# One ring of ten slots for the expert weights of a hybrid encoder block, each item's w_down behind its own gate_up

## The chip, the cores and the metric

One core of one Trainium2 chip. The time is the device time of one execution in microseconds, the median of the runs. Everything is float32.

## What is computed

An encoder block for 256 tokens of width 1024: a Hyena branch and a differential attention, mixed into the residual, then a mixture of experts (32 experts, the best four for each token, SwiGLU), and a final norm. The change is in the mixture of experts and in the loads of its weights:

```python
logits = (hf @ w_router + b_router)
top_val, top_idx = lax.top_k(logits, TOP_K)          # 4 of 32
gates = jax.nn.softmax(top_val, axis=-1)
# for each expert e and the tokens xb routed to it
gu = xb @ w_gate_up[e] + b_gate_up[e]                # 1024 x 2048
gate, up = gu[:, :D_EXPERT], gu[:, D_EXPERT:]
gate = jnp.minimum(gate, 7.0)
up = jnp.clip(up, -7.0, 7.0)
glu = gate * jax.nn.sigmoid(1.702 * gate)
y = ((up + 1.0) * glu) @ w_down[e] + b_down[e]       # 1024 x 1024
out = out.at[row_tok].add(y * wts)
```

For one expert w_gate_up has 8 MB and w_down 4 MB, so all of them are 384 MB that come in once.

## The kernel before, in words

The kernel is written with explicit semaphores; every engine runs its own list of instructions in the order in which it is written, and no planner reorders anything.

**Front.** Up to about 300 us the projections, the Hyena branch, attention and the mix run. Their weights pass through a ring of six slots of 16 KB per partition (`ring`), one 2 MB transfer each, issued by SyncE in the order of the list `blocks`. The last six blocks are two of `w_in` (in8 and in9), `hy`, `att`, and two halves of `mix`.

**Items.** The mixture works on items of up to 64 tokens of one expert. An item of every expert comes first (32 of them), and further items follow only where an expert has more than 64 tokens. Here there are 32 items, taken in pairs, so `n_pairs` is 16 (`w_gate_up` is loaded 128 times). In a pair p, item A is 2p and item B is 2p+1.

For each pair TensorE does these pieces of work (lines of the profile in brackets):

- `gather(p)` (L788): picks the token rows of both items out of `xn` with a selection matrix `Sel`. The result in PSUM banks 7 and 6 is copied to `hTp` by `gathered(p)` (L1480), which signals `ga_sb`.
- `gate_up(p, s)` (L796 for the bias, L806 for 64 MATMULs): four pieces `j` of 2 MB of `w_gate_up`; each piece, when read, counts up `gu_used`.
- `activate` on VectorE (L1431 to L1435) with a sigmoid on ScalarE (L1070), then `act_transpose` on TensorE (L812) and `act_copy` on ScalarE (L1074), which gives `actT`.
- `down` (L824, 32 MATMULs): two pieces of 2 MB of `w_down`, counted by `dn_used`. The result in bank 6 is copied by `y_copy` (L1470) into one half of `y`.
- `place_weights` (L841): transposes the matrix of gate weights `Wt`, which `placed` (L1485) copies to `Pw`.
- `scatter` (L833): adds the pair's rows onto the token sums in banks 0 to 3.

**Order around the change.** Before, `down` runs one item late. In the loop over the pairs 1 to 15 TensorE does: gather(p), gate_up A(p), down of item B of pair p-1, transposes of A, gate_up B(p), scatter of the pair before, down A(p), transposes of B, place_weights. The last down stands behind the loop.

**Slots.** There are ten slots of 2 MB: `gu_a` (four slots of the ring, for the w_gate_up of A), `gu_b` (four slots made of the regions dft, ur and x that the front no longer needs, for the w_gate_up of B) and `dn_row` (two slots of the ring, for every w_down). Each row is refilled as its own piece is read. SyncE's loop issues, in this order, four of gate_up A, two of w_down of B of the pair before, four of gate_up B, two of w_down of A. An issue waits for `gu_used` or `dn_used`, and all that stands behind it in SyncE's list waits too. The last w_down goes in four pieces of 1 MB into `last_row`.

**Loops.** TensorE and SyncE have one loop body for the pairs: TensorE's runs for 1 to 15, SyncE's for 2 to 15, with expert numbers from the table `table_i`. VectorE and ScalarE have a loop for 1 to 15.

Of the kernel before, what the change touches and what calls it, by code (L numbers as in the profile page):

```python
# [33 lines left out]
D = 1024  # L34
# [66 lines left out]
def build(nc, a, out):  # L101
    with ExitStack() as ctx:
# [40 lines left out]
        gu_a = ring[:NJ]  # L143
        gu_b = [span("dft", 0, 4096), span("ur", 4096, 4096), span("ur", 0, 4096), span("x", 0, 4096)]
        dn_row = ring[NJ:NJ + NC]
        last_row = [at("ring", 2048 * c, 2048) for c in range(4)]
        fgB = at("ring", 4096 * 2, D)
        junk = at("ring", 4096 * 3, 2048)
# [104 lines left out]
        def sem(name):  # L253
            return ctx.enter_context(nc.semaphore(name))
# [11 lines left out]
            gu_used dn_used tr_done sc_done ga_done pt_done  # L266
# [4 lines left out]
        s_gua = [sem(f"gate_up_a_in{j}") for j in range(NJ)]  # L271
        s_gub = [sem(f"gate_up_b_in{j}") for j in range(NJ)]
        s_dn = [sem(f"down_in{c}") for c in range(NC)]
# [53 lines left out]
        w_gu, w_dn = a["w_gate_up"], a["w_down"]  # L327
        block = ctx.enter_context(nc.Block())
# [3 lines left out]
        def _(sp):  # L332
# [33 lines left out]
            def gate_up(dst, landed, expert, j):  # L366
# [5 lines left out]
            def down(c, expert):  # L372
                src = w_dn[expert, c] if isinstance(expert, int) else w_dn[bass.ds(expert, 1), c]\
                    .rearrange("o p n -> p (o n)")
                sp.dma_start(dn_row[c], src).then_inc(s_dn[c], 16)


            last_use = {n % 6: n for n in range(len(blocks))}
            for f in sorted(range(6), key=lambda s: last_use[s]):
                if blocks[last_use[f]] == ("mix", 0, 0):  # L380
                    sp.wait_ge(S["s_ps"], 2 * HEADS)
                    gate_up(gu_b[0], s_gub[0], 1, 0)
                    sp.wait_ge(S["pj_sb"], KD)
                    gate_up(gu_b[1], s_gub[1], 1, 1)
                    sp.dma_start(b_down[0:E, :], a["b_down"][0]).then_inc(S["bd_in"], 16)
                wait_used(blocks[last_use[f]])
                if f < NJ:
                    gate_up(gu_a[f], s_gua[f], 0, f)
                else:
                    down(f - NJ, 0)  # L390
            sp.wait_ge(S["mix_ps"], 4)
            gate_up(gu_b[2], s_gub[2], 1, 2)
# [1188 lines left out]
```

## Time and profile before

| | us |
|---|---|
| median of 3 runs | 1252.24 |
| lowest, highest | 1250.06, 1254.26 |
| the profiled execution, whole | 1254.92 |
| its span in the trace | 1253.1 |
| TensorE busy (MATMUL) | 1140.6 |
| VectorE busy | 451.5 |
| ScalarE busy | 116.4 |
| bytes moved | 465.13 MB, 371 GB/s over the span |

The profile divides the span into 40 slices of 31.3 us each. Its chain of work that ended last lists 52% TensorE and 40% transfers of w_gate_up. A share of busy time is a mean over stages that have different limits, so the stages must be read apart. Two hold for this kernel: the front up to about 360 us, and the pairs behind it.

### The profile page before, as it was taken

Reading aid. Unit: us, or ns where it says so; the run is one execution under the profiler, and the core shown is the slowest. Engines: PE = TensorE matmul, PEld = TensorE weight load, DVE = VectorE, ACT = ScalarE, POOL = GpSimd, SP = SyncE. Lnnn points to the kernel's source line nnn. Section 1 sums busy time; section 2 is a strip of 40 time slices with the busy share of each in tenths; the row PEclk is TensorE's granted clock in tenths of the full one; section 3 lists DMA queues with packets and bytes.
Section 4 is the critical chain, followed back from the end, with each engine's and each line's share of the span. In section 5 each row is a group of like instructions: output and inputs, shape, how many; then the busy total and the mean of one; then the engine's idle time right before and its main releaser. Section 6 shows DMA issues by size and latency. Waiting matters only on the chain.

```text
span 1253.1 us, 13746 instructions
## 1 busy us (share of the span) xinstructions
PE 1140.6 (91%) x5333; PEld 521.6 (42%) x5333; DVE 451.5 (36%) x975; ACT 116.4 (9%) x217; POOL 11.8 (1%) x12
## 2 busy tenths in 40 slices
PE   3999999997999999999999999998989898999996
PEld 1588678864333333333232323232333333232322
DVE  3467236527613141432313141313233231313143
ACT  1111122611000000000000000000000000000000
POOL 0000000003000000000000000000000000000000
PEclk9999999998999999999999999999999999999999
DMA  9997941167659999999999999999999999999994
GB/s 341 366 370 303 391 163 68 67 248 292 269 212 429 428 427 429 428 429 428 428 428 429 429 427 428 427 430 429 427 428 427 430 429 427 428 427 430 428 428 190
DMA packets 49025, 465.13 MB, mean 371 GB/s; under 512 B 5466, under 2 KB 6220, under 8 KB 21100
## 3 DMA queue, kind: packets, MB, share of 16 engines
q1 hardware_dynamic: 45592, 461.11, 88.3%
q10 hardware_dynamic: 3412, 3.74, 1.0%
q8 instruction: 13, 0.21, 0.1%
q14 instruction: 8, 0.07, 0.0%
HBM read 463.79 MB, written 1.05 MB: 371 GB/s over the span
## 4 chain that ended last, share of the span: by engine, by line
PE 52%; DMA 40%; DVE 4%; SPq 2%; issue 1%; ACT 1%; DVEq 0%; ACTq 0%
DMA arena<-in_w_gate_up 40%; PE ps L806 12%; PE ps L824 11%; PE ps L566 8%; PE ps L833 5%; PE ps L689 2%; PE ps L712 2%; PE ps L661 2%; PE ps L788 1%; SPq L370 1%; PE ps L560 1%; PE ps L483 1%; PE ps L529 1%; PE ps L796 1%; PE ps L516 1%
## 5 line engine op out<-in xcount | busy, mean ns | idle before, releaser
L806 PE MATMUL ps<-arena 128*64 128x512 f32 x2048 | 455.2, 597 | 33.9 <-DMA arena<-in_w_gate_up 33.9
L806 PEld LDWEIGHTS ps<-arena 128*64 128x64 f32 x2048 | 141.4, 137 | 345.9 <-issue 273.2
L824 PE MATMUL ps<-arena 128*64 128x512 f32 x1024 | 226.0, 594 | 0.7 <-issue 0.7
L1431 DVE TENSOR_SCALAR arena<-ps 128x512 f32<-128x512 f32 x32 | 22.1, 691 | 380.2 <-PE ps L806 380.2
L824 PEld LDWEIGHTS ps<-arena 128*64 128x64 f32 x1024 | 72.1, 137 | 149.3 <-issue 146.0
L1470 DVE TENSOR_TENSOR arena<-ps,arena 64x512 f32<-64x512 f32 x64 | 44.1, 689 | 188.5 <-PE ps L824 188.1
L566 PE MATMUL ps<-arena 128*128 128x256 f32 x448 | 97.7, 380 | 0.0
L566 PEld LDWEIGHTS ps<-arena 128*128 128x128 f32 x448 | 85.1, 190 | 13.8 <-issue 2.6
L1070 ACT ACTIVATE arena<-arena 128x512 f32<-128x512 f32 x32 | 20.1, 630 | 607.3 <-DVE arena L1431 607.3
L788 PE MATMUL ps<-arena 128*128 128x128 f32 x512 | 63.1, 283 | 10.8 <-DVE arena L1485 10.8
L788 PEld LDWEIGHTS ps<-arena 128*128 128x128 f32 x512 | 60.1, 197 | 14.7 <-issue 14.7
L833 PE MATMUL ps<-arena 128*128 128x512 f32 x128 | 59.3, 605 | 1.5 <-DVE arena L1470 1.5
L796 PE MATMUL ps<-arena 32*64 32x512 f32 x256 | 35.3, 621 | 12.9 <-DVE arena L1480 12.9
L1456 DVE TENSOR_SCALAR arena<-arena 128x128 f32<-128x128 f32 x128 | 44.3, 346 | 4.6
L1074 ACT ACTIVATE arena<-ps 128x512 f32<-128x512 f32 x32 | 19.1, 597 | 248.0 <-PE ps L812 248.0
L1480 DVE COPY arena<-ps 128x512 f32<-128x512 f32 x32 | 22.1, 692 | 52.7 <-PE ps L788 52.7
L833 PEld LDWEIGHTS ps<-arena 128*128 128x128 f32 x128 | 23.0, 189 | 37.6 <-issue 35.2
L1445 DVE SCALAR_TENSOR_TENSOR arena<-arena 128x128 f32<-128x128 f32 x96 | 33.8, 352 | 3.4
L661 PE MATMUL ps<-arena 128*128 128x256 f32 x128 | 32.1, 409 | 0.0
L1220 DVE SCALAR_TENSOR_TENSOR arena<-arena 128x2048 f32<-128x2048 f32 x12 | 28.2, 2351 | 3.1 <-DMA arena<-in_w_ada 2.7
L689 PE MATMUL ps<-arena 128*128 128x256 f32 x128 | 28.0, 380 | 0.0
L712 PE MATMUL ps<-arena 128*128 128x512 f32 x64 | 27.8, 593 | 0.0
(240 smaller groups left out, 629.5 us busy)
## 6 DMA issues: line engine op xcount, KB each, us to landing
arena<-in_w_gate_up SPq DMA_DIRECT2D x128, 2048.0 KB, 31.3
arena<-in_w_down SPq DMA_DIRECT2D x62, 2048.0 KB, 23.6
arena<-in_w_ada SPq DMA_DIRECT2D x12, 2048.0 KB, 17.1
arena<-in_w_in SPq DMA_DIRECT2D x10, 2048.0 KB, 16.5
arena<-in_w_mix_out SPq DMA_DIRECT2D x2, 2048.0 KB, 8.9
arena<-in_w_down SPq DMA_DIRECT2D x4, 1024.0 KB, 28.5
arena<-in_w_hy_out SPq DMA_DIRECT2D x1, 2048.0 KB, 15.0
arena<-in_w_attn_out SPq DMA_DIRECT2D x1, 2048.0 KB, 19.0
```

The source lines that it names most:

```text
L566: last = mm(bank(b, 256, c * 256), w[:, k, cc * P:(cc + 1) * P], hT[:, k, :], start=(k == 0), stop=(k == KD - 1))
L661: last = mm(bank(m % 3, 256, (i % 2) * 256), w[:, k, cc * P:(cc + 1) * P], hT[:, k, :], start=(k == 0), stop=(k == KD - 1))
L689: last = mm(bank(pj_bank[i % 4], 256, o), w[:, k, i * P:(i + 1) * P], src[:, k, :], start=(k == 0), stop=(k == CT - 1))
L712: return mm(bank(2 * t + h), merged[:, k, t * P:(t + 1) * P], mix[k // 4][:, k % 4, h * 512:(h + 1) * 512], start=(k == 0), stop=(k == KD ...
L788: last = mm(bank(b, 128, kk * 128), xn[:, t, k * P:(k + 1) * P], Sel[:, t, :], start=(t == 0), stop=(t == TT - 1))
L796: mm(ps[64 * h:64 * h + 64, 4 + b, :], mask[E * b:E * b + E, s, :], sel_bias[E * b:E * b + E, h * 512:(h + 1) * 512], start=True, stop=False)
L806: last = mm(ps[64 * h:64 * h + 64, 4 + b, :], hTp[:, k, s * 64:(s + 1) * 64], w[:, o:o + 512], start=False, stop=(k == KD - 1))
L824: last = mm(ps[64 * h:64 * h + 64, 6, :], lhs, rows[c][:, qq * D + h * 512:qq * D + (h + 1) * 512], start=(q == 0), stop=(q == 7))
L833: last = mm(bank(2 * t + h), Pw[:, t, :], y[:, h * 512:(h + 1) * 512], start=False, stop=stop, skip_group_check=True)
L1445: ins = V.scalar_tensor_tensor(Sel[:, t, :], iota, s, Sel[:, t, :], ALU.is_equal, ALU.add)
L1456: st(V.tensor_scalar(dst[:, t, :], iota, pk[:, k, t:t + 1], gk[:, k, t:t + 1], ALU.is_equal, ALU.mult))
L1470: last = V.tensor_tensor(y[64 * s:64 * s + 64, 512 * h:512 * (h + 1)], ps[64 * h:64 * h + 64, 6, :], gate2B[64 * h:64 * h + 64, 512 * h:51 ...
```

## The change

All ten slots become one ring, `slots`, in the order of use: for each pair four of gate_up A, two of w_down A, four of gate_up B, two of w_down B. Transfer n goes to slot n mod 10. One semaphore, `consumed`, counts the pieces that TensorE has read, in the same order. Down of an item follows its own gate_up: TensorE does gate_up A, scatter of the pair before, transposes of A, down A, gate_up B, gather of the next pair, transposes of B, place_weights, down B. `gathered` for the pairs from 1 on moves from VectorE to ScalarE (`ACT.Copy`). On VectorE, `y_copy` stands ahead of `activate`. The pairs 1 to 14 are written out on TensorE and SyncE, and only pair 15 (and further ones) is in a loop, whose w_down B goes in four pieces of 1 MB into the slots of w_down A of the same pair, in every run of the loop. The first slots are handed to the expert weights in another order: gate_up 0 first, then its w_down, then gate_up 1.

TensorE from the first gate_up on, before (a row `MATMUL x32` in this list stands for 64 MATMULs of the profile, `x16` of L824 and L788 for 32; L855 and L861 add b_down):

```order
L806 MATMUL ps<-arena 64x512 x32
L855 MATMUL ps<-arena 32x128 x2
L861 MATMUL ps<-arena 128x512 x4
L812 MATMUL ps<-arena 128x128 x4
L796 MATMUL ps<-arena 64x512 x4
L806 MATMUL ps<-arena 64x512 x32
L824 MATMUL ps<-arena 64x512 x16
L812 MATMUL ps<-arena 128x128 x4
L841 MATMUL ps<-arena 128x128 x2
```

And after, where the lines are L846 (gate_up), L852 (act_transpose), L864 (down), L835 (bias), L827 (gather), L881 (place_weights):

```order
L846 MATMUL ps<-arena 64x512 x32
L895 MATMUL ps<-arena 32x128 x2
L901 MATMUL ps<-arena 128x512 x4
L852 MATMUL ps<-arena 128x128 x4
L864 MATMUL ps<-arena 64x512 x16
L835 MATMUL ps<-arena 64x512 x4
L846 MATMUL ps<-arena 64x512 x32
L827 MATMUL ps<-arena 128x128 x16
L852 MATMUL ps<-arena 128x128 x4
L881 MATMUL ps<-arena 128x128 x2
L864 MATMUL ps<-arena 64x512 x16
```

Down of expert 0 moved from behind the second gate_up to ahead of it, and the gather of pair 1 stands between the second gate_up and its transposes.

A later pair on TensorE, before (the loop body, without its register instructions):

```order
L806 MATMUL ps<-arena 64x512 x32
L833 MATMUL ps<-arena 128x512 x4
L819 REGISTER_ALU
L824 MATMUL ps<-arena 64x512 x16
L812 MATMUL ps<-arena 128x128 x4
L841 MATMUL ps<-arena 128x128 x2
```

And after (one of the written-out pairs, L873 is scatter):

```order
L835 MATMUL ps<-arena 64x512 x4
L846 MATMUL ps<-arena 64x512 x32
L873 MATMUL ps<-arena 128x512 x4
L852 MATMUL ps<-arena 128x128 x4
L864 MATMUL ps<-arena 64x512 x16
L835 MATMUL ps<-arena 64x512 x4
L846 MATMUL ps<-arena 64x512 x32
L827 MATMUL ps<-arena 128x128 x16
L852 MATMUL ps<-arena 128x128 x4
L881 MATMUL ps<-arena 128x128 x2
L864 MATMUL ps<-arena 64x512 x16
```

Scatter moved from the second gate_up of a pair to the first, and the gather from the pair's start to its second gate_up.

SyncE from the last block of the front on, before:

```order
L360 DMA arena<-in_w_mix_out 128x4x1024 x2
L370 DMA arena<-in_w_gate_up 128x4096 x2
L375 DMA arena<-in_w_down 128x4096 x2
L370 DMA arena<-in_w_gate_up 128x4096 x2
L385 DMA arena<-in_b_down 32x1024
L370 DMA arena<-in_w_gate_up 128x4096 x8
L375 DMA arena<-in_w_down 128x4096 x2
L370 DMA arena<-in_w_gate_up 128x4096 x4
L375 DMA arena<-in_w_down 128x4096 x2
```

And after (L393 is w_gate_up, L399 w_down):

```order
L382 DMA arena<-in_w_mix_out 128x4x1024 x2
L393 DMA arena<-in_w_gate_up 128x4096 x4
L399 DMA arena<-in_w_down 128x4096 x2
L413 DMA arena<-in_b_down 32x1024
L393 DMA arena<-in_w_gate_up 128x4096 x4
L399 DMA arena<-in_w_down 128x4096 x2
L393 DMA arena<-in_w_gate_up 128x4096 x4
L399 DMA arena<-in_w_down 128x4096 x2
```

The w_down of expert 1 now comes ahead of the w_gate_up of expert 2, and each of its transfers waits for a piece of expert 0's gate_up to be read; the number of transfers issued at each place up to there is the same, ten slots and four refills.

The core of the diff:

```diff
+        in8, in9, hy, att, mix0, mix1 = (ring[where[b] % 6] for b in blocks[-6:])
+        slots = [in8, span("dft", 0, 4096), in9, hy, att, span("ur", 4096, 4096), mix0, mix1,
+                 span("ur", 0, 4096), span("x", 0, 4096)]
+        NS = len(slots)
+        A0, DA, B0, DB, PAIR = 0, NJ, NJ + NC, 2 * NJ + NC, 2 * (NJ + NC)
+        FIXED = E // 2 - 1
+        fixed_slot = [(PAIR * FIXED + i) % NS for i in range(DB)]
+        uses_before = [sum(n % NS == k for n in range(PAIR * FIXED)) for k in range(NS)]
+        def place(p, i):
+            if isinstance(p, int):
+                n = PAIR * p + i
+                return slots[n % NS], s_slot[n % NS], 16 * (n // NS + 1)
+            k = fixed_slot[i]
+            return slots[k], s_slot[k], p * 16 + 16 * (uses_before[k] + 1 - FIXED)
...
+            def free(p, i):
+                sp.wait_ge(S["consumed"], used(p, i - NS + 1))
-            def pair_of(p, e_a, e_prev, e_b):
+            def pair_of(p, e_a, e_b):
                 for j in range(NJ):
-                    sp.wait_ge(S["gu_used"], p * 8 + (j - 7))
-                    gate_up(gu_a[j], s_gua[j], e_a, j)
+                    free(p, A0 + j)
+                    gate_up(place(p, A0 + j), e_a, j)
                 for c in range(NC):
-                    sp.wait_ge(S["dn_used"], p * 4 + (c - 3))
-                    down(c, e_prev)
+                    if isinstance(p, int):
+                        free(p, DA + c)
+                    else:
+                        sp.wait_ge(S["consumed"], used(p, c - 1))
+                    down(place(p, DA + c), e_a, c)
                 for j in range(NJ):
-                    sp.wait_ge(S["gu_used"], p * 8 + (j - 3))
-                    gate_up(gu_b[j], s_gub[j], e_b, j)
-                for c in range(NC):
-                    sp.wait_ge(S["dn_used"], p * 4 + (c - 1))
-                    down(c, e_a)
+                    free(p, B0 + j)
+                    gate_up(place(p, B0 + j), e_b, j)
+                if isinstance(p, int):
+                    for c in range(NC):
+                        free(p, DB + c)
+                        down(place(p, DB + c), e_b, c)
+                else:
+                    for c in range(4):
+                        sp.wait_ge(S["consumed"], used(p, DA + c // 2 + 1))
+                        sp.dma_start(piece(c), w_dn[bass.ds(e_b, 1), c // 2, :, 2048 * (c % 2):2048 * (c % 2 + 1)]
+                                     .rearrange("o p n -> p (o n)")).then_inc(s_last[c], 16)
...
+            def down_a(p):
                 pe.wait_ge(S["act_rdy"], p * 2 + 1)
                 act_transpose()
+                pe.wait_ge(S["actT_rdy"], p * 2 + 1)
+                down([place(p, DA + c) for c in range(NC)])
+            def gate_up_b(p):
                 gate_up(p, 1)
+                pe.wait_ge(S["y_rdy"], p * 2 + 1)
+                gather(p + 1)
+            def down_b(p):
+                pe.wait_ge(S["ga_sb"], p * 2 + 3)
                 pe.wait_ge(S["act_rdy"], p * 2 + 2)
                 act_transpose()
                 pe.wait_ge(S["actT_rdy"], p * 2 + 2)
                 pe.wait_ge(S["wt_rdy"], p + 1)
                 place_weights()
+                pe.wait_ge(S["ga_sb"], p * 2 + 4)
...
+            def pair_of(p):
+                pe.wait_ge(S["mask_rdy"], p + 1)
+                gate_up(p, 0)
+                pe.wait_ge(S["y_rdy"], p * 2)
+                pe.wait_ge(S["pt_sb"], p)
+                scatter(False)
+                down_a(p)
+                gate_up_b(p)
+                down_b(p)
+            for p in range(1, FIXED):
+                pair_of(p)
+            with pe.Fori(FIXED, n_pairs) as p:
+                pair_of(p)
...
+            def gathered(p):
+                for half in range(2):
+                    act.wait_ge(S["ga_done"], p * 2 + (half + 1))
+                    A(hTp[:, 4 * half:4 * half + 4, :].rearrange("p k s -> p (k s)"), ps[:, 7 - half, :], ACT.Copy)\
+                        .then_inc(S["ga_sb"], 1)
+            def pair_of(p):
+                sigmoid(p * 2)
+                act_copy(p * 2)
+                sigmoid(p * 2 + 1)
+                gathered(p + 1)
+                act_copy(p * 2 + 1)
```

## Rows read from the trace of the kernel before

**Rows 1.** The page: busy time by engine, and GB/s in 40 slices.

```profile
PE 1140.6 (91%) x5333; PEld 521.6 (42%) x5333; DVE 451.5 (36%) x975; ACT 116.4 (9%) x217; POOL 11.8 (1%) x12
...
GB/s 341 366 370 303 391 163 68 67 248 292 269 212 429 428 427 429 428 429 428 428 428 429 429 427 428 427 430 429 427 428 427 430 429 427 428 427 430 428 428 190
```

**Rows 2.** Chain of waits, two of 11 alike: start us, us, what.

```profile
878.91 41.95 DMA arena<-in_w_gate_up
...
937.64 41.96 DMA arena<-in_w_gate_up
```

**Rows 3.** Timeline of TensorE, one early pair: start us, us, instructions [idle <-releaser].

```profile
419.64 3.83 PE L788 MATMUL ps<-arena 128*128 128x128 f32 x32 [0.70 <-DVE arena L1485]
...
446.61 1.09 PE L796 MATMUL ps<-arena 32*64 32x512 f32 x8
447.63 13.95 PE L806 MATMUL ps<-arena 128*64 128x512 f32 x64
461.51 3.71 PE L833 MATMUL ps<-arena 128*128 128x512 f32 x8
465.15 7.09 PE L824 MATMUL ps<-arena 128*64 128x512 f32 x32
472.17 0.66 PE L812 MATMUL ps<-arena 128*128 128x128 f32 x4
473.51 0.44 PE L841 MATMUL ps<-arena 128*128 128x128 f32 x2 [0.69 <-ACT arena L1074]
474.70 0.48 PE L788 MATMUL ps<-arena 128*128 128x128 f32 x2 [0.75 <-DVE arena L1485]
```

**Rows 4.** Stretches of 5 us: each engine busy, PEclk, DMA share, GB/s.

```profile
335.00:340.00 5.00, 5.00 (x20) 1.62 (x18) 4.20 (x11) 1.83 (x3) 0.00 (x0) 0.91 1.02 436
340.00:345.00 5.00, 5.00 (x22) 1.61 (x20) 4.01 (x13) 0.00 (x0) 0.00 (x0) 0.75 0.92 393
345.00:350.00 5.00, 5.00 (x26) 1.67 (x24) 0.00 (x0) 0.00 (x0) 0.00 (x0) 1.00 0.00 0
...
355.00:360.00 5.00, 5.00 (x26) 1.68 (x24) 2.77 (x4) 0.63 (x1) 0.00 (x0) 1.00 0.25 46
360.00:365.00 5.00, 3.46 (x19) 1.42 (x16) 2.03 (x4) 0.60 (x1) 0.00 (x0) 1.00 0.85 341
```

**Rows 5.** Timeline of SyncE, issue of the 15th transfer.

```profile
358.67 0.33 SPq L375 DMA_DIRECT2D arena<-in_w_down  x1
```

**Rows 6.** Timeline of all engines, from expert 0's activation on.

```profile
337.98 0.66 PE L812 MATMUL ps<-arena 128*128 128x128 f32 x4
...
338.68 0.60 ACT L1074 ACTIVATE arena<-ps 128x512 f32<-128x512 f32 x1 [2.44 <-PE ps L812]
...
340.07 15.13 PE L806 MATMUL ps<-arena 128*64 128x512 f32 x64
...
355.03 7.03 PE L824 MATMUL ps<-arena 128*64 128x512 f32 x32
```

**Rows 7.** Timeline of all engines, at the end.

```profile
1214.61 3.65 PE L806 MATMUL ps<-arena 128*64 128x512 f32 x16 [1.25 <-DMA arena<-in_w_gate_up]
...
1218.32 0.69 DVE L1431 TENSOR_SCALAR arena<-ps 128x512 f32<-128x512 f32 x1 [10.16 <-PE ps L806]
...
1220.50 0.69 DVE L1435 TENSOR_TENSOR arena<-arena 128x512 f32<-128x512 f32 x1
...
1231.29 7.09 PE L824 MATMUL ps<-arena 128*64 128x512 f32 x32 [0.65 <-issue]
...
1238.42 1.39 DVE L1470 TENSOR_TENSOR arena<-ps,arena 64x512 f32<-64x512 f32 x2 [7.32 <-PE ps L824]
```

**Rows 8.** Stretches of 2.5 us at the end, columns as in rows 4.

```profile
1232.50:1235.00 2.50, 2.50 (x14) 0.89 (x12) 0.00 (x0) 0.00 (x0) 0.00 (x0) 1.00 0.43 175
```

**Rows 9.** w_gate_up transfers between 700 and 1100: issue to landing.

```profile
DMA to landing us min/median/max: 26.9/34.4/42.0
```

**Rows 10.** The page: instruction queue, packets, MB, share of 16 engines.

```profile
q8 instruction: 13, 0.21, 0.1%
```

More of the change, by code:

```diff
@@ L142, in build @@
         NJ, NC = 4, 2
[L143 to L148, printed above, removed]
         y = b_down = span("prm", 0, D)
@@ L327, in build, with piece, used @@
         w_gu, w_dn = a["w_gate_up"], a["w_down"]
+        in8, in9, hy, att, mix0, mix1 = (ring[where[b] % 6] for b in blocks[-6:])
[12 more added lines that the diff above has]
+            return slots[k], s_slot[k], p * 16 + 16 * (uses_before[k] + 1 - FIXED)
+        def piece(c):
+            return slots[fixed_slot[DA + c // 2]][:, 2048 * (c % 2):2048 * (c % 2 + 1)]
+        def used(p, i):
+            return p * PAIR + i
+        fgB = slots[fixed_slot[A0]][:, 0:D]
+        junk = slots[fixed_slot[A0 + 1]][:, 0:2048]
         block = ctx.enter_context(nc.Block())
@@ L370, in gate_up, with down @@
                 sp.dma_start(dst, src).then_inc(landed, 16)
-            def down(c, expert):
+            def down(place_, expert, c):
+                dst, landed, _ = place_
                 src = w_dn[expert, c] if isinstance(expert, int) else w_dn[bass.ds(expert, 1), c]\
                     .rearrange("o p n -> p (o n)")
[L375 to L390, printed above, removed]
+                sp.dma_start(dst, src).then_inc(landed, 16)
+            wait_used(blocks[-6])
+            gate_up(place(0, 0), 0, 0)
+            sp.wait_ge(S["s_ps"], 2 * HEADS)
+            gate_up(place(0, 1), 0, 1)
+            wait_used(blocks[-5])
+            gate_up(place(0, 2), 0, 2)
+            wait_used(blocks[-4])
+            gate_up(place(0, 3), 0, 3)
+            down(place(0, DA), 0, 0)
+            sp.wait_ge(S["pj_sb"], KD)
+            down(place(0, DA + 1), 0, 1)
+            sp.dma_start(b_down[0:E, :], a["b_down"][0]).then_inc(S["bd_in"], 16)
+            wait_used(blocks[-2])
+            gate_up(place(0, B0), 1, 0)
+            wait_used(blocks[-1])
+            gate_up(place(0, B0 + 1), 1, 1)
             sp.wait_ge(S["mix_ps"], 4)
-            gate_up(gu_b[2], s_gub[2], 1, 2)
+            gate_up(place(0, B0 + 2), 1, 2)
             sp.wait_ge(S["res_ps"], 1)
@@ L413, in expert_of @@
             def expert_of(index):
                 return sp.value_load(table_i[0:1, bass.ds(index, 1)], min_val=0, max_val=E - 1)
-            pair_of(1, 2, 1, 3)
+            for c in range(NC):
+                free(0, DB + c)
+                down(place(0, DB + c), 1, c)
+            for p in range(1, FIXED):
+                pair_of(p, 2 * p, 2 * p + 1)
             sp.wait_ge(S["tables"], 2)
             n_pairs = sp.value_load(table_i[0:1, 48:49], min_val=E // 2, max_val=ITEMS // 2)
-            with sp.Fori(2, n_pairs) as p:
-                pair_of(p, expert_of(p * 2), expert_of(p * 2 - 1), expert_of(p * 2 + 1))
+            with sp.Fori(FIXED, n_pairs) as p:
+                pair_of(p, expert_of(p * 2), expert_of(p * 2 + 1))
@@ L813, in act_transpose, with down @@
                 last.then_inc(S["tr_done"], 1)
-            def down(landed, rows, count):
-                n = KD // len(rows)
-                for c in range(len(rows)):
-                    pe.wait_ge(landed[c], count)
+            def down(pieces):
+                n = KD // len(pieces)
+                for c, (rows, landed, count) in enumerate(pieces):
+                    pe.wait_ge(landed, count)
                     for qq in range(n):
@@ L1476, in gathered @@
                     v.wait_ge(S["ga_done"], p * 2 + (half + 1))
-                    if half and isinstance(p, int):
+                    if half:
                         v.wait_ge(S["ex_ps"], 1)
```

130 lines of the change are left out of this document (50 added, 80 removed).

## The prediction

> **What bounds the kernel now.** I read the page first: TensorE is busy for 91% of the span, yet from slice 13 of 40 on the GB/s row stands at 427 to 430 in every slice [rows 1]. Both could be the limit, so the next view is the chain of waits, in order of time. It goes, once in each pair of experts, through one wait for a w_gate_up transfer of 42 us, and these waits are 58.73 us apart [rows 2]. A pair moves 12 transfers of 2 MB (8 of w_gate_up, 4 of w_down), 25.17 MB, and 25.17 MB in 58.73 us is 428 GB/s: one transfer every 4.895 us. Early on, while TensorE is still behind, the same pair takes 55.06 us from gather to gather (419.64 to 474.70) [rows 3]. So TensorE needs 55 us for what the stream delivers in 58.7 us, and after some 530 us it only follows the stream. From there the end is: the moment from which the stream runs without a hole, plus the bytes that are left at 428 GB/s, plus what is computed after the last byte.
>
> The moment is what matters. The table of 5 us stretches shows DMA shares of 0.92, 0.00, 0.25 and 0.85 for 340-345, 345-350, 355-360 and 360-365 (350-355 reads 0.00 too) [rows 4]. That is 0.4 + 5 + 5 + 3.75 + 0.75 = 14.9 us in which the engines of the stream stand still. SyncE issues the next w_down at 358.67 [rows 5], because its destination is the slot of expert 0's w_down, and TensorE reads that only from 355.03 on, after the whole gate_up of expert 1 (340.07 to 355.2) [rows 6]. By then 14 of the 192 transfers (counting 2 MB each) are in: ten slots filled, and the first four refilled. The other 178 follow without a hole.
>
> At the end, the last w_gate_up piece lets its matmuls start at 1214.61, the last down runs from 1231.29 to 1238.4, and the stream is dry at about 1233.6 (share 0.43 in 1232.5-1235) [rows 7, 8]. From the end of the last down to the end of the span are 14.7 us.
>
> **1. The hole at 345 closes: -14.5 us.** The change lets down of expert 0 follow its own gate_up. The transposes L812 start at 337.98, the copy L1074 ends at 338.68 + 0.60 = 339.28 [rows 6], so down can start at 339.35. Half of it, 16 of 32 matmuls, frees a slot: 3.5 us by 7.09 us for 32 [rows 3]. The granted clock here is 0.91 and then 0.75 of full on average over 335-345 [rows 4], and the 64 matmuls of L806 at 340.07 took 15.13 us [rows 6] where they take 13.95 otherwise [rows 3], so add up to 1.2 us. The slot is free at 342.9 to 344.1, while the stream is busy with the four refills until 344.6. The queue never runs dry, or for a fraction of a microsecond until the first packets flow. Of 14.9 us, 13.4 to 14.9 are recovered; I take 14.5.
>
> Does the hole come back later? In a ring of ten, transfer n (from 0) needs use n-10 read. With the stream running from 345.0, transfer 16 wants to start at 355 and needs the first piece of expert 1's gate_up read: down ends at 347.4, four bias matmuls and 16 matmuls later it is 352. Transfer 20 wants 374.4 and needs the first half of expert 1's down: gate_up ends at 362.5, gather 3.83, transposes, copy and place_weights 2.2, half a down 3.5, so 372. Transfer 26 wants 403.8 and needs expert 2's down: 399. The margin is about 3 us in each place, and later grows by 3.9 us a pair (next part). That margin covers the estimate; if it were used up, the hole would be as large as the excess.
>
> **2. TensorE's pair in the new order: 54.8 us, nothing on the path.** The work is the same; what differs is which matmuls cover the activation. Expert A: bias and gate_up 14.9 (446.61 to 461.51), scatter 3.64, transposes to the end of the copy 1.34 (472.17 to 473.51), down 7.02 [rows 3]. Expert B: 14.9, gather 3.83, 1.34, place_weights and its successor 0.44 to 1.09 (0.8), down 7.02 [rows 3]. Sum 54.8 us, against 58.73 us of the stream. VectorE's chain L1431 to L1435 takes 2.9 us (1218.32 to 1220.50 + 0.69) [rows 7]; scatter's 3.64 and gather's 3.83 cover it. If they did not, 2.9 us twice in a pair would still only reach 60.6. The two copies of the gathered rows go from VectorE to ScalarE, 0.6 us each by L1074 [rows 6]; the second one ends behind the gather and ahead of the activation's copy, which puts some tenths on the switch. All of it lies under waits for the stream, once the first pairs are over.
>
> SyncE passes its queue in the order of use: in the last pair w_down waits for the last down of the pair before, and the four half pieces wait for down of expert 30. Behind each of these waits at least four transfers are in flight, 19.6 us, while the waiting takes under 10 us. Up to 42 us from issue to landing (8.6 transfers) are there already before the change [rows 9], so the deeper queue is not new.
>
> **3. The tail: +2.7 us.** Before, four w_down transfers follow the last w_gate_up piece (experts 30 and 31); after, only the two of expert 31. So the last w_gate_up piece comes 2 x 4.895 = 9.8 us later against the stream: 1224.4 where it was 1214.6. Then 16 matmuls 3.6, the gather 3.85 (issued for a pair that doesn't exist), transposes and copy 1.34, place_weights 0.8, down 7.1: its end is 1241.1, where it was 1238.4. The last quarter of w_down, in at 1233.6 as before, isn't waited for. Bounds 2.3 and 3.0 by the two values for place_weights. Before, the 9.4 us of scatter, down and switch lay between; they now lie ahead of it.
>
> **4. Code: +2.0 us.** Fourteen pairs are written out on TensorE where before one loop body served. Each has 258 MATMULs and as many weight loads. Before, the 5333 MATMULs [rows 1] come from 5333 - 14 x 258 = 1721 written ones, and the page lists 13 packets of 0.21 MB on the instruction queue [rows 10]: one packet of 16 KB for 132 of them. So 27 packets more, 0.44 MB, which is 1.0 us of the stream's rate. A packet occupies one of the 16 engines: 0.1% of 16 x 1253 us (0.05 to 0.15) over 13 packets is 0.8 to 2.3 us. Spread over all engines 27 of them cost 1.4 to 3.9 us. I take 2.0, near the lower end and to the plain rate. Below nothing it can't go, since the stream holds all the old bytes too; the lower bound is 0.
>
> The Trainium skill (Runtime: NRT & Kernel Launch, Instruction fetch mechanics) says the sequencer fetches its code in blocks of 16 KiB over a queue of its own and that the cost of crossing a block is "mostly hidden". The 13 packets of 0.21 MB agree with the size; by the word "hidden" this term would be 0 and the time 1240. That stays inside the forecast's own range. The skill (DMA: Bandwidth & Descriptors, queues and rings) also has each DMA engine take turns between its queues packet by packet, so that a fetch would take its own time out of one engine's stream; no run here shows yet how fetches spread over the engines.
>
> **Sum.** -14.5 + 2.7 + 2.0 = -9.8 us. The profiled execution took 1254.92 us (span 1253.1, 1.8 around it), so 1245.1 for its like; it lies 2.7 above the median of 1252.24, so the median goes to 1242.4. With the bounds: -14.9 + 2.3 + 0 = -12.6 and -13.4 + 3.0 + 3.9 = -6.5, so 1239.6 to 1245.7. The stream's rate reads between 427 and 430 from slice to slice, 0.35% either way of 871 us, so 3 us more on both sides.
>
> **Rivals.**
> Fetches fall on one engine (slower). With a share of 1.0 and one transfer behind the other, each transfer must be spread over all 16 engines, and it is in when the slowest has done its part. If the 27 extra packets always take the same engine, that one is late by 27 x 0.8 = 22 to 62 us. At 1 us a packet: -11.8 + 27 = +15, 1267. It decides from 0.44 us of stream per packet on (11.8 / 27). For it: the packets are few, one queue. Against it, weakly: the slices right behind the last written-out code (13 and 14, 429 and 428) read no lower than the later ones [rows 1]. A mix (four or five engines) would give +6 in place of +2, 1246 to 1248.
>
> TensorE becomes the bound (no gain). If the switches expose the chain wholly, the pair is 54.8 + 5.8 = 60.6, which is 1.9 us x 14 = 26 us over the stream, less 11.8: 1266. With half of it, 57.7, nothing shows. Break-even at 59.6 us a pair (58.73 + 11.8 / 14). Against it: the covers of 3.64 and 3.83 stand in the rows.
>
> The hole moves (gain partly lost). If the margins of 3 us are misjudged by 8 us in one of the first pairs, 5 us come back: 1247; if they are missed in several, within 0.3%.
>
> The change gives the full 14.5 with a free tail and free code: 1238.
>
> **Chances.** Forecast (1237 to 1247) 0.70; the full gain 0.05; the mix or a moved hole 0.11, of which 0.06 end at 1246 to 1248.5 and 0.05 within 0.3% of before; one engine slowed 0.10 and TensorE the bound 0.04, which together give 0.11 slower and 0.03 within 0.3%. 0.3% is 3.8 us, about what this kernel's measurement can tell from no change: faster means under 1248.5, slower over 1256. So faster 0.81, the same 0.08, slower 0.11. The range 1237 to 1252 leaves out the slower cases and the last part of the full gain.
>
> **What will show it.** The table of 5 us stretches should have DMA share near 1.0 from 325 on through 345-365; if a hole stands there, step 1 fails. SyncE's issue of the 15th transfer should come at 343 to 344. In the steady part pairs should be 58.7 to 58.9 us apart; 60 or more is the code or TensorE, told apart by whether TensorE waits for w_gate_up (code) or VectorE and ScalarE (the switch). The instruction queue should list about 40 packets. From the end of the last w_gate_up matmuls to the end of the last down should be 13 us. Wrong altogether would be a GB/s row below 425 in the middle slices.

## Result and the profile after

| | median us | lowest, highest |
|---|---|---|
| before | 1252.01 | 1250.06, 1254.26 |
| changed | 1243.70 | 1242.74, 1244.79 |

The ratio is 0.9933, interval 0.9914 to 0.9953, so 8.3 us faster. In a later comparison the changed kernel took 1244.93 against 1251.99, ratio 0.9943 (0.993 to 0.9956). The profiled execution of the changed kernel took 1242.74, with a span of 1240.9.

The page of the changed kernel (busy time, GB/s, instruction queue), which answers to [rows 1, 10]:

```profile
PE 1133.0 (91%) x5365; PEld 519.7 (42%) x5365; DVE 427.9 (34%) x945; ACT 133.8 (11%) x249; POOL 11.8 (1%) x12
...
GB/s 341 369 398 305 394 146 68 136 208 270 277 417 429 428 427 428 428 428 426 427 430 427 426 429 427 428 428 426 428 427 429 428 427 427 428 427 427 429 424 135
...
q8 instruction: 42, 0.69, 0.2%
```

The slice that read 212 GB/s before reads 417. TensorE's share is the same 91%, and says nothing of what changed.

The 5 us stretches of the changed kernel (from, to and length in us, busy time of TensorE, its weight loads, VectorE, ScalarE and GpSimd, granted clock, DMA share, GB/s, as in [rows 4]):

```profile
335.00:340.00 5.00, 5.00 (x18) 1.41 (x16) 4.44 (x14) 0.00 (x0) 0.00 (x0) 0.71 0.98 419
340.00:345.00 5.00, 5.00 (x28) 1.39 (x26) 1.38 (x2) 0.00 (x0) 0.00 (x0) 1.00 0.82 292
345.00:350.00 5.00, 5.00 (x26) 1.67 (x24) 0.00 (x0) 0.00 (x0) 0.00 (x0) 1.00 1.02 436
350.00:355.00 5.00, 5.00 (x26) 1.64 (x24) 0.00 (x0) 0.00 (x0) 0.00 (x0) 1.00 1.00 429
355.00:360.00 5.00, 5.00 (x32) 2.70 (x29) 1.65 (x3) 0.63 (x1) 0.00 (x0) 1.00 0.99 423
360.00:365.00 5.00, 4.26 (x32) 3.00 (x33) 1.69 (x4) 1.68 (x3) 0.00 (x0) 1.00 1.01 433
```

A hole is best counted in the bytes that are missing, since a starting stream has a share before it has its rate. At 428 GB/s six stretches would sum to 2568. Here they sum to 2432, and 136 / 428 x 5 = 1.6 us are missing. Before, the same six sum to 1216 (436, 393, 0, 0, 46, 341), which is 15.8 us. So 14.2 us came back.

TensorE of the changed kernel around that place, and at the end of the program, and SyncE's issue of the 15th transfer:

```profile
314.99 13.95 PE L846 MATMUL ps<-arena 128*64 128x512 f32 x64
...
334.70 8.63 PE L864 MATMUL ps<-arena 128*64 128x512 f32 x32 [0.69 <-ACT arena L1123]
```

```profile
339.95 3.76 SPq L393 DMA_DIRECT2D arena<-in_w_gate_up  x2
```

```profile
1210.13 3.65 PE L846 MATMUL ps<-arena 128*64 128x512 f32 x16 [1.25 <-DMA arena<-in_w_gate_up]
1213.72 3.84 PE L827 MATMUL ps<-arena 128*128 128x128 f32 x32
1217.39 0.60 PE L852 MATMUL ps<-arena 128*128 128x128 f32 x4
1218.73 0.44 PE L881 MATMUL ps<-arena 128*128 128x128 f32 x2 [0.74 <-ACT arena L1123]
1219.10 7.09 PE L864 MATMUL ps<-arena 128*64 128x512 f32 x32
```

**The zero of the clock.** The front before the experts is the same in both kernels, but it does not end at the same time in every execution. The first 64 MATMULs of gate_up start at 319.61 before and at 314.99 in this execution; in the second profiled execution of the same changed kernel they start at 320.39, and its span is 1246.2. From that start to the end of the span are 925.9 and 925.8 us. So I compare this rest, span less start, which repeats within 0.1 us where whole executions differ by 5 (within 0.6 us in the two traces of a kernel of experiment 5, 923.2 and 923.8). The kernel before has one trace. Before it is 1253.1 - 319.61 = 933.5. The change moved it by -7.6.

### The profile page after: what moved, and what is told of

Same layout as the page of the kernel before. It is cut to its first block, busy times and chain, and to the rows that moved or that the text cites. A ratio compares the mean times of both kernels' runs of the same rounds, so it can differ in the third digit from the quotient of the medians.

```text
span 1240.9 us, 13121 instructions
## 1 busy us (share of the span) xinstructions
PE 1133.0 (91%) x5365; PEld 519.7 (42%) x5365; DVE 427.9 (34%) x945; ACT 133.8 (11%) x249; POOL 11.8 (1%) x12
## 4 chain that ended last, share of the span: by engine, by line
PE 60%; DMA 33%; DVE 3%; ACT 2%; SPq 1%; issue 1%; DVEq 0%; ACTq 0%
DMA arena<-in_w_gate_up 31%; PE ps L846 18%; PE ps L864 13%; PE ps L605 8%; PE ps L827 5%; DMA arena<-in_w_ada 2%; PE ps L728 2%; PE ps L751 2%; PE ps L873 2%; PE ps L700 2%; PE ps L835 1%; PE ps L599 1%; ACT arena L1123 1%; ACT arena L1130 1%; PE ps L881 1%; PE ps L640 1%
## 5 line engine op out<-in xcount | busy, mean ns | idle before, releaser
L846 PE MATMUL ps<-arena 128*64 128x512 f32 x2048 | 454.8, 596 | 36.5 <-DMA arena<-in_w_gate_up 36.3
L846 PEld LDWEIGHTS ps<-arena 128*64 128x64 f32 x2048 | 140.8, 137 | 348.3 <-issue 274.1
L864 PE MATMUL ps<-arena 128*64 128x512 f32 x1024 | 228.3, 599 | 11.0 <-ACT arena L1123 11.0
L864 PEld LDWEIGHTS ps<-arena 128*64 128x64 f32 x1024 | 71.1, 138 | 146.5 <-issue 131.7
L605 PE MATMUL ps<-arena 128*128 128x256 f32 x448 | 97.7, 379 | 0.0
L605 PEld LDWEIGHTS ps<-arena 128*128 128x128 f32 x448 | 84.9, 190 | 14.0 <-issue 2.5
L827 PEld LDWEIGHTS ps<-arena 128*128 128x128 f32 x544 | 63.8, 196 | 13.4 <-issue 13.4
L827 PE MATMUL ps<-arena 128*128 128x128 f32 x544 | 67.0, 283 | 0.0
L873 PE MATMUL ps<-arena 128*128 128x512 f32 x128 | 59.3, 605 | 1.5 <-DVE arena L1526 1.5
L873 PEld LDWEIGHTS ps<-arena 128*128 128x128 f32 x128 | 23.0, 189 | 37.6 <-issue 35.3
L835 PE MATMUL ps<-arena 32*64 32x512 f32 x256 | 34.8, 612 | 1.2 <-DVE arena L1536 1.2
L700 PE MATMUL ps<-arena 128*128 128x256 f32 x128 | 29.0, 380 | 0.0
L728 PE MATMUL ps<-arena 128*128 128x256 f32 x128 | 28.0, 379 | 0.0
L728 PEld LDWEIGHTS ps<-arena 128*128 128x128 f32 x128 | 24.2, 190 | 3.2
L700 PEld LDWEIGHTS ps<-arena 128*128 128x128 f32 x128 | 23.8, 190 | 2.9
## 6 DMA issues: line engine op xcount, KB each, us to landing
arena<-in_w_hy_out SPq DMA_DIRECT2D x1, 2048.0 KB, 14.9
```

The costliest lines, as they stand in the source:

```text
L605: last = mm(bank(b, 256, c * 256), w[:, k, cc * P:(cc + 1) * P], hT[:, k, :], start=(k == 0), stop=(k == KD - 1))
L700: last = mm(bank(m % 3, 256, (i % 2) * 256), w[:, k, cc * P:(cc + 1) * P], hT[:, k, :], start=(k == 0), stop=(k == KD - 1))
L728: last = mm(bank(pj_bank[i % 4], 256, o), w[:, k, i * P:(i + 1) * P], src[:, k, :], start=(k == 0), stop=(k == CT - 1))
L827: last = mm(bank(b, 128, kk * 128), xn[:, t, k * P:(k + 1) * P], Sel[:, t, :], start=(t == 0), stop=(t == TT - 1))
L835: mm(ps[64 * h:64 * h + 64, 4 + b, :], mask[E * b:E * b + E, s, :], sel_bias[E * b:E * b + E, h * 512:(h + 1) * 512], start=True, stop=False)
L846: last = mm(ps[64 * h:64 * h + 64, 4 + b, :], hTp[:, k, s * 64:(s + 1) * 64], w[:, o:o + 512], start=False, stop=(k == KD - 1))
```

## Experiments

**1. The order alone.** In the kernel before, only pair 0's down of expert 0 is put ahead of the second gate_up; the slots stay in rows.

```diff
-            gate_up(0, 1)
             pe.wait_ge(S["actT_rdy"], 1)
             down(s_dn, dn_row, 16)
+            gate_up(0, 1)
```

> The kernel before, with one part of the change alone: in the first pair, down of expert 0 stands ahead of the gate_up of expert 1. The ten slots stay split into 4 + 4 + 2. Theory A (the split of the slots, not the order alone, makes the hole): w_down of expert 1 is now issued near 344 and the hole at 345 closes, but after it and four w_gate_up transfers (6 x 4.9 = 29 us, to about 374) the next transfer in SyncE's list is a w_down again, whose slot is read only by the down of expert 1, near 388. So a hole of about 14 us appears at 375 to 389 and the time stays within 2 us of before, about 1252. Rival B (the order alone brings the gain): no hole comes back, the stream starts 14 us earlier, and with the tail of before the time is 1238.

Measured: 1258.43 against 1252.29, ratio 1.0047 (1.0032 to 1.0061). Its stretches, and SyncE's next w_down:

```profile
340.00:345.00 5.00, 5.00 (x28) 1.50 (x28) 1.25 (x4) 0.00 (x0) 0.00 (x0) 1.00 0.82 269
...
370.00:375.00 5.00, 4.21 (x30) 2.29 (x30) 0.79 (x2) 0.00 (x0) 0.00 (x0) 0.97 0.53 223
375.00:380.00 5.00, 5.00 (x26) 1.63 (x24) 0.00 (x0) 0.00 (x0) 0.00 (x0) 1.00 0.00 0
380.00:385.00 5.00, 5.00 (x26) 1.65 (x24) 0.00 (x0) 0.00 (x0) 0.00 (x0) 1.00 0.00 0
385.00:390.00 5.00, 5.00 (x26) 1.71 (x24) 2.45 (x4) 0.63 (x1) 0.00 (x0) 1.00 0.00 0
390.00:395.00 5.00, 5.00 (x28) 1.77 (x28) 1.00 (x2) 0.11 (x1) 0.00 (x0) 1.00 0.65 210
```

```profile
390.88 3.76 SPq L375 DMA_DIRECT2D arena<-in_w_down  x2
```

```profile
362.85 0.66 PE L812 MATMUL ps<-arena 128*128 128x128 f32 x4 [2.97 <-DVE arena L1435]
...
365.59 6.06 PE L788 MATMUL ps<-arena 128*128 128x128 f32 x32 [0.71 <-DVE arena L1485]
```

The hole at 345 is gone and one of 20 us stands 30 us later, where the two slots of w_down wait for down of expert 1 behind another gate_up. The rest behind the start is 939.2, 5.7 longer than before; the missing bytes grow from 15.8 to 21.8 us (1.8 before 350 and 20.0 from 370 to 400), which accounts for it. Down behind its own gate_up closes no hole by itself in this slot plan. Theory A had the hole right and its size wrong (14 us, 1252 in time). Measured from the start of the experts, down of expert 1 comes 6.2 us later than before: nothing stands any more between gate_up and transposes of expert 1, so TensorE waits 2.97 us for its activation, and the gather behind it takes 6.06 us in place of 3.83 (granted clock 0.50 in 365-370, which is 1.2 GHz). So the uncovered activation makes up most of the 6 us; the hole that comes back would cost about what the first one did.

**2. The ring without the new order in pair 0.** In the changed kernel, pair 0 keeps the old work order (VectorE's order in that pair follows it), and the ring brings its transfers in the order in which that uses them.

```diff
-                n = PAIR * p + i
+                n = PAIR * p + (i if p else LATE[i])
...
-            down_a(0)
-            gate_up_b(0)
+            pe.wait_ge(S["act_rdy"], 1)
+            act_transpose()
+            gate_up(0, 1)
+            pe.wait_ge(S["actT_rdy"], 1)
+            down([place(0, DA + c) for c in range(NC)])
```

`LATE` is (0, 1, 2, 3, 8, 9, 4, 5, 6, 7, 10, 11).

> The changed kernel, with the first pair in the old order of work: gate_up of expert 1 ahead of down of expert 0, and the ring and its list in that order too. Theory A (the ring alone closes the hole, since the next slot to be read is always the next to be filled): transfer 15 waits for the first piece of expert 1's gate_up, read near 340 + 3.9 = 344 on the clock of before, and the stream has no hole over 2 us there; time within 1.5 us of the changed kernel, 1243 to 1245. Rival B (down right behind its gate_up is what is needed): a hole of 10 us or more at 340 to 360, time 1252 or more.

Measured: 1247.82 against 1252.29, ratio 0.9947 (0.993 to 0.9965). Its stretches:

```profile
345.00:350.00 5.00, 5.00 (x26) 1.61 (x24) 0.00 (x0) 0.00 (x0) 0.00 (x0) 1.00 0.80 269
350.00:355.00 5.00, 5.00 (x26) 1.68 (x24) 0.00 (x0) 0.00 (x0) 0.00 (x0) 1.00 1.04 446
```

No hole beyond the same 1.7 us, and 926.4 behind its start, 0.5 longer than the changed kernel. Its median lies above the expected range; its profiled execution started the experts at 319.8, so most of that is the front, though I can't show this for the executions without a trace. Together with experiment 1: the ring, with slots filled and freed in the order of use, closes the hole, and the place of expert 0's down does not matter to it. In the ring the 15th transfer needs a piece of gate_up read, whichever work comes first.

**3. Nearly no written-out pairs.** FIXED from 15 to 1, so every pair from 1 on is in the loop.

```diff
-        FIXED = E // 2 - 1
+        FIXED = 1
```

> The changed kernel with all pairs from 1 on in the loop. The least code (about 13 packets), but w_down A of each pair waits for the last down of the pair before while TensorE is still some 28 us behind. Theory A (the ring in the order of use matters until TensorE has caught up): holes in the stream in the pairs 1 to 3, 12 us or more in sum, and a time of 1249 or more. Rival B (order of use matters only in the first pair): 1240.

Measured: 1259.81 against 1251.90, ratio 1.0065 (1.0038 to 1.0092), the slowest of all. The instruction queue lists 14 packets in place of 42. Stretches and SyncE:

```profile
350.00:355.00 5.00, 5.00 (x26) 1.72 (x24) 0.00 (x0) 0.00 (x0) 0.00 (x0) 1.00 0.70 298
355.00:360.00 5.00, 5.00 (x24) 1.44 (x21) 0.00 (x0) 0.00 (x0) 0.00 (x0) 1.00 0.00 0
360.00:365.00 5.00, 4.28 (x38) 4.04 (x36) 2.90 (x5) 2.31 (x4) 0.00 (x0) 1.00 0.00 0
365.00:370.00 5.00, 4.99 (x24) 1.84 (x26) 0.42 (x1) 0.00 (x0) 0.00 (x0) 1.00 0.02 5
```

```profile
369.21 3.76 SPq L399 DMA_DIRECT2D arena<-in_w_down  x2
```

In the loop the w_down of A waits not for the slot ten transfers back but for down of the pair before (`used(p, c - 1)`): 369.2 is the middle of down of expert 1. From 335 to 380 the bytes of 19.2 us are missing, 3.4 more than before. With the tail (+2.1) and 15 pairs at 0.15 (experiment 5) that gives +7.8; measured are 941.2 - 933.5 = +7.7. So the written-out pairs are there for the early waits, not for TensorE.

**4. The price of code.** In the kernel before, TensorE's pairs 1 to 14 (or 1 to 7) are written out, nothing else.

```diff
-            with pe.Fori(1, n_pairs) as p:
+            def pair_of(p):
...
+            for p in range(1, 15):
+                pair_of(p)
+            with pe.Fori(15, n_pairs) as p:
+                pair_of(p)
```

> The kernel before, with TensorE's loop written out for the pairs 1 to 14, and nothing else. 27 to 29 more instruction packets. Theory A (fetching the code takes stream time, as the 59.1 us a pair of the changed kernel against 58.73 suggests): pairs of about 59.1 us, +4 to +5 us, 1256 to 1257. Rival B (fetches hidden): pairs stay at 58.73, time 1252. Rival C (only their bytes count): +1.0 us, 1253.

> The kernel before, with TensorE's pairs 1 to 7 written out and 8 to 15 in the loop: half the dose of the run that wrote out 14 (+5.1 us, 59.1 us a pair). Theory A (each packet of code costs stream time): about 27 to 28 packets on the instruction queue, +2.5 us, pairs 8 to 15 back at 58.73 us apart. Rival B (the cost is that of having more code, whenever it runs, or of the first pairs only): all of the +5 or none, or pairs 8 to 15 slow too.

Measured: 14 pairs 1257.36 against 1252.29, ratio 1.0033 (1.0020 to 1.0046), 42 packets; 7 pairs 1255.85 against 1251.90, ratio 1.0022 (1.0008 to 1.0035), 28 packets. The chain of waits with 14 pairs written, and then with 7, of which the first three rows here belong to written pairs:

```profile
700.11 42.73 DMA arena<-in_w_gate_up
759.63 41.94 DMA arena<-in_w_gate_up
818.36 42.40 DMA arena<-in_w_gate_up
```

```profile
584.99 42.88 DMA arena<-in_w_gate_up
644.66 42.55 DMA arena<-in_w_gate_up
704.00 41.93 DMA arena<-in_w_gate_up
762.72 41.95 DMA arena<-in_w_gate_up
```

Written pairs are 59.1 us apart on average, looped ones 58.74. By the medians 29 packets cost 5.1 us, 0.18 each, and 15 cost 3.9, 0.26 each (the interval allows 0.07 to 0.29); by the rest behind the start they cost 5.5 and 1.8, 0.19 and 0.12 each.

The trace holds more than these sums. The semaphore of a 2 MB transfer counts up 16 times, once as each sixteenth of it lands, and every count has its time. In the kernel before, the last count of a transfer comes 2.0 to 2.2 us behind the first, from 407 us to the end, and both repeat every 4.895 us. With written-out pairs each code packet moves exactly one of the 16 counts back by 1.53 us, and the other 15 stay within 0.03 us. Followed from transfer to transfer in the kernel with 14 pairs, it is one of the same eight counts each time, in the same order, three and a half times round. The other eight lose nothing, and the first count still comes every 4.895 us. But a transfer is in when its last count is, so the stream that TensorE sees moves back by as much as the slowest of the eight: 1.53 us for a round of eight packets, 0.19 each. From 407 us to the last w_gate_up the last counts lose 5.6 us with 14 pairs written (28 packets in that stretch; first to last count grows from 2.0 to 7.6 us), 2.0 us with 7 (14 packets, to 4.0 us) and 0.1 us in the kernel before. That is the rest behind the start within 0.2 us, and it says why 15 packets cost less each: a packet costs nothing where it meets a sixteenth that is not the slowest.

**5. Fewer written pairs in the changed kernel.** FIXED = 10, then FIXED = 5.

```diff
-        FIXED = E // 2 - 1
+        FIXED = 5
```

> The changed kernel with the pairs 1 to 9 written out and 10 to 15 in the loop (before: 1 to 14 and 15). In the loop both w_down of a pair use the same two slots, so w_down A waits for the last down of the pair before; by then TensorE follows the stream and four or more transfers are in flight. Theory A (29 packets of code cost 4.5 us, 0.16 us each): 10 packets fewer, -1.6 us, 1242; pairs 10 to 15 at 58.73 us apart. Rival B (the code costs nothing): unchanged, 1243.7. Rival C (the loop's wait makes holes): each pair of the loop 2 us or more longer, 1250 or more.

> The changed kernel with the pairs 1 to 4 written out and 5 to 15 in the loop, on all engines' lists of TensorE and SyncE. 21 packets of code fewer. TensorE is then still behind the stream when the loop begins, by about 9 us at pair 5 (it gains 4.7 us a pair and has caught up in pair 6 or 7), and w_down A of the loop waits for the last down of the pair before, behind which 16 us of transfers are in flight. Theory A (code 0.18 us a packet, wait covered): -3 us against the changed kernel, less about 1 us for the quarters of w_down that the loop moves in 1 MB pieces (58.85 against 58.74 us a pair in the run with 10), so 1241 to 1242. Rival B (the lag is larger than that cover): holes of several us in the pairs 5 and 6, 1245 or more. Rival C (code isn't what costs): 1244.

Measured: 1244.42, ratio 0.9927 (0.9911 to 0.9944), 32 packets; 1244.05, ratio 0.9932 (0.9911 to 0.9952), 22 packets. Theory A had 1242 and 1241 to 1242; the medians show no gain over the changed kernel. Part of the reason is in the chain of the second one:

```profile
934.87 40.42 DMA arena<-in_w_gate_up
993.76 40.46 DMA arena<-in_w_gate_up
```

The looped pairs are 58.88 us apart, not 58.74. A looped pair brings 4 of its 25 MB in four transfers of 1 MB. One more kernel tells whether the pieces cost that: it brings them in two transfers of 2 MB.

```diff
-                    for c in range(4):
-                        sp.wait_ge(S["consumed"], used(p, DA + c // 2 + 1))
-                        sp.dma_start(piece(c), w_dn[...]).then_inc(s_last[c], 16)
+                    for c in range(NC):
+                        sp.wait_ge(S["consumed"], used(p, DA + c + 1))
+                        down((slots[fixed_slot[DA + c]], s_last[c], None), e_b, c)
```

> The kernel with the pairs 5 to 15 in the loop, and w_down B in the loop in two transfers of 2 MB instead of four of 1 MB. Theory A (1 MB pieces cost 0.1 us a pair): 58.74 us a pair in the loop, 1 us under the run with four pieces, 1240 to 1241; the last down starts 9 us after the last w_gate_up piece is in, when the first 2 MB are in, so the tail doesn't change. Rival B (pieces cost nothing): the same as the run with four.

Measured: 1242.76 against 1251.90, ratio 0.9923 (0.9902 to 0.9943). Its chain:

```profile
932.02 40.28 DMA arena<-in_w_gate_up
990.77 40.31 DMA arena<-in_w_gate_up
```

58.74 us apart again. The pieces cost 0.14 us a pair, 1.5 us in the 11 looped pairs of FIXED = 5, whose rest behind the start is 924.8. Without the pieces it is 923.2 us, 2.7 less than in the changed kernel, for 20 packets fewer: 0.13 each. By the last counts of the transfers the stream loses 1.6 us here and 4.75 in the changed kernel, 3.1 less.

**6. The last pair apart.** On top of that kernel, the loops end one pair earlier. The last pair is written once more on every engine: the stream brings gate_up 30, gate_up 31, down 30, down 31, and TensorE works in that order, without the gather for a pair that doesn't exist. The kernel below it and the changed kernel ran again beside it.

```diff
+            gate_up(q, 0)
...
+            scatter(False)
...
+            act_transpose()
+            gate_up(q, 1)
...
+            down([place(q, DA + c) for c in range(NC)])
...
+            act_transpose()
...
+            place_weights()
...
+            down(late)
```

> The kernel with pairs 1 to 4 of TensorE written out, 5 to 14 in a loop, and the last pair (experts 30 and 31) apart on every engine: the stream brings w_gate_up of 30, w_gate_up of 31, w_down of 30, w_down of 31, and TensorE does gate_up 30, scatter, gate_up 31, down 30, down 31, without the gather for a pair that doesn't exist. Theory A (the tail is what TensorE does behind the last w_gate_up, and the stream paces the rest): the last w_gate_up piece comes two transfers (9.8 us) earlier against the stream, behind it stand 3.6 + down 30 (7.1) + transposes and copy, about 3.4 with place_weights, + down 31 (7.1) = 21 to 22.6 us in place of 16.1, so the end of down comes 3.3 to 4.9 us earlier: 1238 to 1240 where the same kernel with the last pair in the loop is at 1242.8. Rival B (the tail is set by the last byte: its transfer, the last 16 matmuls and the output): the last w_down is waited for, and nothing or under 1 us is gained: 1242 to 1243.

> The kernel with pairs 1 to 4 of TensorE written out and 5 to 15 in a loop, the last w_down in two transfers, once more, to stand beside the kernel with the last pair apart on the same chip. If its time follows from the stream it comes again at 1242.8 +- 1; if the 1 us that it stood under the changed kernel was chance, it comes at 1243.7.

> The changed kernel itself, once more on the same chip: 1243.7 +- 1. The front before the experts differs from execution to execution by 1 to 5 us; the median of five rounds should show less of it.

Measured: 1241.70 for the last pair apart, ratio 0.992 (0.9907 to 0.9934); 1241.64 without that, ratio 0.9928 (0.9915 to 0.994); 1244.93 for the changed kernel, ratio 0.9943 (0.993 to 0.9956). The end with the last pair apart:

```profile
1199.48 3.65 PE L859 MATMUL ps<-arena 128*64 128x512 f32 x16 [0.38 <-DMA arena<-in_w_gate_up]
1204.47 3.65 PE L877 MATMUL ps<-arena 128*64 128x512 f32 x16 [1.34 <-DMA arena<-in_w_down]
1209.28 3.65 PE L877 MATMUL ps<-arena 128*64 128x512 f32 x16 [1.16 <-DMA arena<-in_w_down]
1212.87 0.66 PE L865 MATMUL ps<-arena 128*128 128x128 f32 x4
1214.21 0.44 PE L894 MATMUL ps<-arena 128*128 128x128 f32 x2 [0.69 <-ACT arena L1159]
1214.58 3.65 PE L877 MATMUL ps<-arena 128*64 128x512 f32 x16
1219.06 3.65 PE L877 MATMUL ps<-arena 128*64 128x512 f32 x16 [0.83 <-DMA arena<-in_w_down]
```

Three of the four pieces of w_down are now waited for, the last one too: that is what the end of rival B looks like. Its forecast of under 1 us doesn't hold in the traces, where the rest behind the start is 920.2 against 923.2 and 923.8 without it, 3.0 to 3.6 shorter. The medians show no difference, 0.06 us. So a gain of 3 us in the part that was changed is seen in one execution, and in the time of the kernel it isn't shown. Both versions are some 2 to 3 us below the changed kernel on the same chip, with intervals that overlap.

## Why the prediction held, point by point

The forecast was 1242.4 and the median 1243.7, inside the likeliest case. The sum had -9.8 and it came to -7.6; most of the difference is the code, which came to more than twice its forecast.

**The hole: -14.5 forecast, -14.2 measured.** That these agree within 0.3 us is in part luck: by its missing bytes the hole was 15.8 us and not 14.9, and 1.6 us of it stay where 0 to 1.5 were allowed and 0.4 taken. In the changed kernel the mechanism is the one forecast: the 15th transfer follows the first half of expert 0's down (334.70 to about 339.3) and is issued at 339.95. Moved by the 4.62 us between the two starts of the experts, that is 344.6 on the clock of [rows 4], where 343 to 344 was the sign. Down took 8.63 us in place of 7.09; the granted clock of that stretch is 0.71 of full, a mean of 1.2 and 2.4 GHz, behind the short MATMULs and waits of the switch. The 14th transfer lands from 340.19 to 341.02, so the issue at 339.95 is 0.2 us ahead of the first of the 16 counts; the next one lands 6.5 us behind it and not 4.9, and that is the 1.6 us. What the prediction didn't ask is which part of the change closes the hole. Experiments 1 and 2 show that it is the ring: the new order alone moves the hole and costs 6 us, and the ring closes it with the old order in pair 0 as well. The margins of 3 us behind it held: no later stretch shows a hole.

**TensorE's pair: 54.8 forecast, 54.05 measured.** While TensorE is still behind, the 64 MATMULs of gate_up A start at 371.58 and, one pair later, at 425.63:

```profile
371.58 8.80 PE L846 MATMUL ps<-arena 128*64 128x512 f32 x40
```

```profile
425.63 13.95 PE L846 MATMUL ps<-arena 128*64 128x512 f32 x64
```

Scatter and gather covered the activation as worked out. TensorE's waits for the copy ahead of down A come to 11.0 us in 16 pairs, 0.69 each, which the sum held in its 1.34. The rival in which TensorE becomes the bound fell.

**The tail: +2.7 forecast, +2.1 measured.** From the start of the last 16 MATMULs of gate_up (1210.13) to the end of down (1226.2) are 16.1 us where 16.7 stood. Before, it was 23.8 [rows 7]. Less the 9.8 us of two transfers: 16.1 + 9.8 - 23.8 = +2.1. From the end of those MATMULs (1213.7) to the end of down are 12.5, where 13 was given as the sign. The 9.4 us of scatter, down and switch named in that step are not in the rows (1218.26 to 1231.29 are 13.0 [rows 7]); they enter no sum.

**Code: +2.0 forecast, +4.5 measured.** This is the mis-sized term. The remainder is -7.6 + 14.2 - 2.1 = +4.5; the last counts of the transfers lose 4.75 us in the changed kernel by themselves, and experiment 4 gives 5.1 for as many packets in the kernel before. With the 0.1 us that they lose before the change too, hole, tail and code sum to -14.2 + 2.1 + 4.6 = -7.5 where -7.6 was measured, so nothing is left for the copies that changed their engine or place, which no run tries by themselves. The number of packets was right (29 more, 27 forecast), and so was the kind. Wrong was the step from the rows to the price: I took the plain bytes and a spread over all 16 engines, 0.07 us a packet, and measured are 0.17 here and 0.19 in experiment 4. The even share can be read from the changed kernel itself, from the queue's line for 700 to 1100 us:

```profile
q8 instruction: 14, 0.23, 0.2%
```

0.2% (0.15 to 0.25) of 16 x 400 us over 14 packets is 0.7 to 1.1 us on one engine, 0.04 to 0.07 us if all 16 share it. The stream lost two to four times as much, for two reasons that the 16 counts show: a packet sets its sixteenth of the stream back by 1.53 us (even over 16 that is 0.10 us), and the packets go round eight sixteenths and not 16 (1.53 / 8 = 0.19). For the pairs the sign stood at 58.7 to 58.9; the written pairs came 59.1 apart:

```profile
753.24 42.68 DMA arena<-in_w_gate_up
812.06 43.87 DMA arena<-in_w_gate_up
872.06 42.83 DMA arena<-in_w_gate_up
931.02 42.59 DMA arena<-in_w_gate_up
```

Some pairs take 1.2 us more (812.06 to 872.06), most take 0.1 to 0.2 more. In the long pairs a packet meets the sixteenth that is already the slowest: the last counts step back by 1.3 us at 585, 1.2 at 807 and 1.3 at 1039, every eighth packet, and by 0.2 at most for any other; from 407 us to the end the first and last count move from 1.7 to 6.7 us apart. No row names the engine behind a sixteenth. The rival of all packets on one engine, from 0.44 us of stream each on, fell: less than half of that was measured. Its mechanism, the transfer that waits for its slowest engine, was the true one, and what the mix of four or five engines would give (+6) was closer to the truth than the even spread.

The Trainium skill (Runtime: NRT & Kernel Launch, Instruction fetch mechanics) calls the cost of crossing a block "mostly hidden". By experiment 4 it isn't where the DMA engines are full: 5.1 us for 29 packets. No wait of TensorE there is put down to its code; the weights come later.

**The signs together.** The 15th transfer, the packets, the 13 us and the GB/s row came out within a few per cent, and the pairs did not; that last sign named the term that was off.

## What to carry to other kernels

When a saturated stream feeds the bound engine, give its buffers out in the order of use from one ring: two rows that are refilled by kind make the whole queue wait for the slower kind, and a new work order only moves the hole. A packet of code sets back one part of that stream, and a transfer waits for its slowest part, so code costs a full stream more than its even share, here 0.14 to 0.20 us for 16 KB: write out only the iterations whose waits differ (here 4 of 14), and check what a looped body waits for in its first run. Compare kernels from the first common event behind the change's start where the part ahead of it varies.

## What the hardware showed beside it

- Code packets: 16 KB each, about 1.07 us from start to end in the trace. Each sets one sixteenth of a full stream back by 1.53 us, one of eight in turn, and the others by nothing: 0.14 to 0.20 us of the stream each over 14 or 28 packets, where their bytes at 428 GB/s are 0.04. The sixteenths do not even out again: 2 us apart at 407 us, 7.6 at 1216 (experiment 4). The loop body of a whole TensorE pair, 258 MATMULs with their weight loads, ran 15 times with 14 packets in all (experiment 3), so it is not fetched again in each run.
- Transfers of 1 MB in place of 2 MB for 4 of 25 MB: 58.88 in place of 58.74 us.
- The depth of the queue did not matter. The median from issue to landing of w_gate_up is 31.3 us before, 41.0 in the changed kernel and 27.7 in the kernel of 1242.76, each with the stream at 428 GB/s.
- The front of the same program ends 5.4 us apart in two executions (314.99 and 320.39), which is two thirds of what the change brings.
